# Two steps of attention values at a time, and a routing table ahead of two conditioning products

## The reference, cut to what matters

```python
    order = jnp.argsort(flat_e)
    ...
    xb = h_pad[slot_tok].reshape(n_blocks, MOE_BLOCK, d)
    def run_block(args):
        xe, e = args
        return (jax.nn.silu(xe @ w_gate[e]) * (xe @ w_up[e])) @ w_down[e]
```

```python
def ada_mod(cond, w, b):
    m = jnp.dot(jax.nn.silu(cond), w) + b
    return jnp.split(m, 3, axis=-1)
```

```python
p = softmax(MLA_SCALE * (q_nope . k_nope + q_rot . k_rot))   # over 1280 keys
o = p @ v                                                    # 64 columns a head
```

## Time and profile before

| | |
|---|---|
| median of 3 runs | 2509.48 us (2509.85, 2502.32, 2509.48) |
| the profiled execution's own time | 2505.39 us |
| its span | 2503.5 us |
| mean granted TensorE clock | 0.959 |
| TensorE busy | 2298.8 us, 92% |
| VectorE busy | 1526.8 us, 61% |
| ScalarE busy | 1186.9 us, 47% |
| GpSimd busy | 373.4 us, 15% |

### The profile page before, as it was taken

The page is one execution under the profiler, slowest core; times in us unless marked ns, Lnnn a source line. Parts: engine busy times, 40 slices in busy tenths (PEclk is TensorE's granted clock), DMA queues, the critical chain, the costliest instruction groups (busy, mean ns, idle before and its releaser), DMA issues.

```text
span 2503.5 us, 27157 instructions
## 1 busy us (share of the span) xinstructions
PE 2298.8 (92%) x10924; PEld 1710.5 (68%) x10924; DVE 1526.8 (61%) x1874; ACT 1186.9 (47%) x1666; POOL 373.4 (15%) x258
## 2 busy tenths in 40 slices
PE   6998789798699999999989999898999998899998
PEld 5766565475388888888768876654555467688876
DVE  5776257543699999999881125846455647533475
ACT  3255246521388888888753154425444522312221
POOL 2000012000111111111100000011555633000014
PEclk9999899899799999999989998998999999999999
DMA  3201010115899999999761110010000032111131
GB/s 119 67 19 49 0 68 1 68 76 215 354 362 387 379 387 396 394 393 378 303 207 50 49 35 1 1 38 1 1 4 31 17 126 76 52 52 51 55 156 51
DMA packets 100953, 342.19 MB, mean 137 GB/s; under 512 B 23356, under 2 KB 48741, under 8 KB 73176
## 3 DMA queue, kind: packets, MB, share of 16 engines
q1 hardware_dynamic: 89176, 318.89, 33.9%
q0 software_dynamic: 10448, 17.28, 1.9%
q10 hardware_dynamic: 1200, 4.24, 0.4%
HBM read 323.54 MB, written 33.60 MB: 143 GB/s over the span
## 4 chain that ended last, share of the span: by engine, by line
PE 81%; DVE 10%; ACT 5%; DMA 3%; issue 1%; SPq 0%; DVEq 0%; POOL 0%; ACTq 0%; POOLq 0%
PE psm L230 77%; DVE mem L953 1%; PE psm L1722 1%; ACT mem L1143 1%; DMA mem<-in_ada_w_dram 1%; PE psm L1073 1%; DVE r L337 1%; DMA mem<-in_w_in_dram 1%; DVE mem L2735 1%; ACT mem L1109 1%; PE psm L1745 1%; PE psm L464 1%; DMA mem<-in_odd_w_out_dram 1%; DVE small L3002 0%; PE psm L1442 0%
## 5 line engine op out<-in xcount | busy, mean ns | idle before, releaser
L230 PE MATMUL psm<-r,r 128*128 128x512 f32 (+3 forms) x7294 | 1750.4, 398 | 77.6 <-DVE r L337 18.0
L230 PEld LDWEIGHTS psm<-r,r 128*128 128x128 f32 (+2 forms) x7294 | 1371.9, 191 | 453.5 <-issue 61.7
L337 DVE TENSOR_TENSOR r<-mem,r 128x1024 fp32r<-128x1024 f32 x448 | 526.1, 1222 | 185.9 <-ACT r L328 180.8
L328 ACT ACTIVATE r<-mem 128x1024 fp32r<-128x1024 f32 x448 | 441.7, 1053 | 34.6 <-DMA mem<-in_w_in_dram 22.2
L230 PE MATMUL psm<-mem 128*64 128x128 f32 (+13 forms) x2230 | 357.9, 437 | 35.1 <-ACT mem L816 10.1
L230 PEld LDWEIGHTS psm<-mem 128*64 128x64 f32 (+6 forms) x2230 | 168.3, 163 | 156.7 <-issue 88.7
L3210 POOL TENSOR_TENSOR mem<-mem 128x1024 f32<-128x1024 f32 x63 | 153.9, 2443 | 176.3 <-ACT mem L3165 175.6
L3165 ACT ACTIVATE mem<-psm 128x512 f32<-128x512 f32 x160 | 95.3, 596 | 145.7 <-PE psm L230 138.2
L3002 DVE TENSOR_REDUCE small<-psm 128x1 f32<-128x1280 f32 x64 | 95.3, 1489 | 102.4 <-PE psm L230 102.2
L230 PE MATMUL psm<-mem,cst 128*128 128x512 f32 (+4 forms) x274 | 114.0, 634 | 23.9 <-ACT mem L924 5.5
L265 ACT ACTIVATE small<-small 128x1 f32<-128x1 f32 (+3 forms) x26 | 7.7, 295 | 236.8 <-DVE small L374 151.6
(11 more groups left out here) (338 smaller groups left out, 1745.9 us busy)
## 6 DMA issues: line engine op xcount, KB each, us to landing
mem<-in_exp_w_gate_dram SPq DMA_DIRECT2D x64, 1024.0 KB, 7.5
mem<-in_exp_w_up_dram SPq DMA_DIRECT2D x64, 1024.0 KB, 7.8
mem<-in_exp_w_down_dram SPq DMA_DIRECT2D x64, 1024.0 KB, 7.3
mem<-in_ada_w_dram SPq DMA_DIRECT2D x16, 1024.0 KB, 14.3
mem<-in_odd_w_in_dram SPq DMA_DIRECT2D x10, 1024.0 KB, 5.4
mem<-in_even_w_in_dram SPq DMA_DIRECT2D x9, 1024.0 KB, 5.4
mem<-in_x_dram SPq DMA_DIRECT2D x16, 512.0 KB, 7.2
mem<-in_w_in_dram SPq DMA_DIRECT2D x8, 1024.0 KB, 5.3
```

The costliest lines, as they stand in the source:

```text
L230: return p.e.matmul(o, l, r, start=start, stop=stop, skip_group_check=True)
L328: p.e.activation(h, mem(kb + 8, [R * n])[:, w * q:w * q + w], ACT.Copy).then_inc(*self.hi_done.up(i, q))
L337: p.e.tensor_tensor(l, mem(kb + 8, [R * n])[:, w * q:w * q + w], h.bitcast(F32), SUB).then_inc(*self.lo_done.up(i, q))
```

## The change

Four things move; no product, copy or DMA is added or taken away.

1. `latent_tensor` multiplies the values of two steps at a time, at odd steps only: at odd t those of t - 3 and t - 2, then the sums that are due.
2. As the sums may come a step later, ScalarE's and VectorE's work at the end of each half (L3173 to L3190) moves from step t = 13, 23, ... to t = 14, 24, ...
3. On TensorE the router's "pos" and "tot" stand ahead of conditioning product 8, and the table ahead of products 10 and 11.
4. On ScalarE the last `ada_rows` stands behind the splits of weight pieces 0 and 1. On GpSimd the clearing of the second gather buffer, which waits for product 11, stands behind the first gather.

```diff
@@ norm2_tensor
-            ada_tensor(p, 4, 9)
+            ada_tensor(p, 4, 8)
@@ router_scalar
-            for g in range(3):
+            for g in range(2):
                 ada_rows(p, g)
@@ rows_pool
-            p.wait_ge(*ada_pe.at(11))
-            p.e.memset(XGB[1], 0.0).then_inc(*moe_pool.up(1))
@@ experts_pool
             gather(p, 0)
+            p.wait_ge(*ada_pe.at(11))
+            p.e.memset(XGB[1], 0.0).then_inc(*moe_pool.up(1))
             gather(p, 1)
@@ experts_scalar
-            for i in range(3):
+            for i in range(2):
                 WE.split_scalar(p, i)
+            ada_rows(p, 2)
+            WE.split_scalar(p, 2)
@@ latent_tensor
-                if 0 <= t - 2 < 80:
-                    values_tensor(p, t - 2)
-                if 0 <= t - 3 < 80 and STEPS[t - 3][2] in (4, 9):
-                    sums_tensor(p, t - 3)
+                if t % 2:
+                    for k in (t - 3, t - 2):
+                        if 0 <= k < 80:
+                            values_tensor(p, k)
+                    for k in (t - 4, t - 3):
+                        if 0 <= k < 80 and STEPS[k][2] in (4, 9):
+                            sums_tensor(p, k)
@@ latent_scalar and latent_vector (the same index in each of their lines)
-                if 0 <= t - 4 < 80 and STEPS[t - 4][2] == 9:
+                if 0 <= t - 5 < 80 and STEPS[t - 5][2] == 9:
@@ tensor
-            ada_tensor(p, 9, 12)
+            ada_tensor(p, 8, 10)
             table_tensor(p)
+            ada_tensor(p, 10, 12)
```

More of the change, by code:

```diff
@@ L3167, in latent_scalar @@
                     beside_scalar(p, t)
-                if 0 <= t - 4 < 80 and STEPS[t - 4][2] == 9:
-                    hp, half, i = STEPS[t - 4]
-                    p.wait_ge(*ml_pe.at("sum", t - 4))
+                if 0 <= t - 5 < 80 and STEPS[t - 5][2] == 9:
+                    hp, half, i = STEPS[t - 5]
+                    p.wait_ge(*ml_pe.at("sum", t - 5))
                     if hp + half:
@@ L3182, in latent_vector @@
                     beside_vector(p, t)
-                if 0 <= t - 4 < 80 and STEPS[t - 4][2] == 9:
-                    hp, half, i = STEPS[t - 4]
+                if 0 <= t - 5 < 80 and STEPS[t - 5][2] == 9:
+                    hp, half, i = STEPS[t - 5]
                     y = YM[:, hp, 512 * half:512 * half + 512]
-                    p.wait_ge(*ml_pe.at("pv", t - 4))
+                    p.wait_ge(*ml_pe.at("pv", t - 5))
                     p.wait_ge(*ml_act.at("r", hp, half))
```

## The result

| | before | after |
|---|---|---|
| median of 4 runs each | 2507.97 us (2502.32 to 2509.85) | 2490.48 us (2489.08 to 2492.07) |
| ratio | | 0.9935, 95% interval 0.9918 to 0.9952 |
| profiled execution: own time / span | 2505.39 / 2503.5 us | 2492.07 / 2490.2 us |
| TensorE busy | 2298.8 us | 2292.1 us |
| latent attention, first scores to first product behind it | 280.47 us | 268.62 us |

A forecast was written before the change was run, and what follows sets the result against it. TensorE, busy for 92% of the span, was taken as the bound. Attention -9 and routing -2 gave -11 us: 2494.4 from the profiled execution, 2498.5 from the median, middle 2496 us, range 2486 to 2508.

The forecast's parts named there:

- Part 2, the stalls: Latent attention: the long TensorE waits at steps 25 and 45 go, -5.9 us each; steps 61 to 68 give -1.2.
- Rival A: Attention: the stalls only move, one long wait with low clock returning per twenty steps; about 2508 us, chance 0.21.
- Part 1, pairs with items: Attention: a pair with two items takes 6.47 us against 6.34, +3.4 us over 26 pairs; the start loses 0.9.
- the item by that pace is 0.58, and 0.19 us is the switch to values: Attention, item to values: of 0.77 us the item takes 0.58, leaving a 0.19 us switch that pairing saves.
- Two zeros of part 1: Attention: pairing values changes nothing in seven pairs with tops, nor in the last ten steps, there within 1 us.
- Weight loads between sets of values: Attention: by a skill rule the second set waits for its load, about 4 us worse; measured rows showed less.
- Part 3, the routing: Router to first expert: moving the table earlier starts the first expert product at 673 to 675, -2 us.
- an earlier first product is worth its whole lead: Experts: TensorE bounds them from the first product on, so that product's lead, -2 us, counts in full.
- it follows the one-hot matrices within 1 to 2 us: Router: the table comes 1 to 2 us behind the one-hot matrices, so indices are ready about 7.5 us earlier.
- Product 10 at 654 keeps the DMA of piece 3 where it is: Between router and experts: conditioning product 10, at 654, leaves the DMA of weight piece 3 unmoved; effect nothing.
- Rival C: Attention: 0.46 us waits in 26 pairs lower TensorE's clock, making the kernel slower, about 2522 us; chance 0.09.
- Rival B: Attention: the short waits are hidden, pairs gain 0.33 us each instead of losing 0.13; about 2484 us, chance 0.10.

The follow-up runs named there:

- vector_shift_only: The kernel before, with only VectorE's division and gate at the end of a half one step later; 2491.15 us (one run), attention 267.16 us.
- items_apart: The kernel after, with the two items of a pair on either side of the two sets of values; 2496.19 us, ratio 0.9962, attention 270.82 us.
- mixed_ten_first: The kernel after, with values paired only where no item waits and the table behind conditioning product 10; 2488.00 us, ratio 0.9930.
- warm_table: The kernel after, with three spare fp32 products filling TensorE's idle time ahead of the table; 2491.84 us, ratio 0.9942.
- ten_first: The kernel after, with the table behind conditioning product 10 instead of 9; 2488.93 us, ratio 0.9931.
- single_ten_first: The kernel after, with values one step at a time and the table behind conditioning product 10; 2488.70 us, ratio 0.9934, attention 267.19 us.
- routing_only: The kernel before, with only the new routing order and the attention unchanged; 2504.88 us, ratio 0.9996, attention 283.42 us.
- after_again: The kernel after, unchanged, run again beside later kernels on the same chip; 2490.72 us, ratio 0.9943, attention 268.64 us.
- pairs_only: The kernel before, with only the values two steps at a time and the end of a half unmoved; 2513.39 us, ratio 1.0038, attention 288.43 us.
- warm_table_rows_first: The kernel after, with three spare products ahead of the table and ScalarE's last conditioning rows ahead of the weight splits; 2489.12 us, ratio 0.9928.
- shift_only: The kernel before, with only the end of a half one step later on ScalarE and VectorE; 2493.45 us, ratio 0.9955, attention 267.18 us.

## Why the prediction came out, step by step

**Part 2, the stalls: right in mechanism and size.** Two times -5.9 us was the term. Ten undisturbed steps, from tops to tops, take 33.77 us in before and 34.07 in after. Those with steps 25 and 45 took 39.75 us each in before, 6.0 over that, and take 34.07 in after, nothing over it: -6.0 each. Those with steps 61 to 68 took 36.17 us and take 34.98, so what they are over went from 2.4 to 0.9 us: -1.5 (predicted -1.2). vector_shift_only shows the cause directly. Rival A did not come: from step 4 on no wait is over 0.54 us.

**Part 1, pairs with items: right.** A pair was to take 6.47 us; it takes 6.46. The start was to lose 0.9 and lost 0.86. But the two parts of the difference were both put too high, by 0.25 and 0.29 us, and cancel: the saving was put at 0.33 (0.19 ahead of the values, 0.14 behind) and is 0.08 by items_apart, and the wait was put at 0.46 and is 0.17 in the profile. The step that failed is "the item by that pace is 0.58, and 0.19 us is the switch to values". The whole interval from item to item, 2.43 us at steps 1 and 2, holds both, and since it went into the sum as measured, the sum came out right. The row itself had said 0.20 us of wait.

**Two zeros of part 1: mis-sized.** The pairs with tops were counted as 0: a pair of steps with tops takes 6.46 us instead of 6.62, so -0.16 in each of seven, -1.1. The step that failed is "only the values' place changes": two sets of values in a row save their 0.15 us there too, and no item waits. The last ten steps were counted as 0, less than 1 us either way: five pairs take 5.13 instead of 5.22 us, and a wait of 0.43 us on ScalarE's exponential is gone; with it -1.1 in all. Together they are most of the difference between the predicted -9 and the measured -11.85 us; the rest is some 0.4 us in the stalls and 0.4 us in the pairs. mixed_ten_first confirms these sizes: without the pairs with items the attention is 265.01 us, 2.2 shorter than with no pairs, which is the -1.1 twice; with them it is 3.6 longer, which is 26 x 0.11 plus 0.86 (over ten steps a pair with items costs 0.11 us more than two single steps).

**Weight loads between sets of values.** Two sets of values take 1.87 us from start to start, against 2.02 for two apart. The prediction weighed the rule of the Trainium skill's page "TensorE: Matmul & The Clock Gate", section "The mechanism", by which a load into row groups in use would wait. The second set costs less than the first, so no wait as after a switch shows here, as three sets in a row had told.

**Part 3, the routing: the first product right, its path wrong in three places, its worth wrong.** The first product came at 673.48, inside 673 to 675, and -2 us was predicted where the trace gives -2.6. But of the lead, 1.7 us outlives the first expert and only 0.3 to 0.5 us shows at the attention. The step that failed there is "an earlier first product is worth its whole lead": half of it goes into products at the lower clock, and where the rest goes stays open. The path:
- The table: "it follows the one-hot matrices within 1 to 2 us" failed. It takes 5 us, and the gather is issued at 660.5 instead of about 657, because TensorE idles 3.06 us and then works at 1.2 GHz (0.50 to 0.51). The clock was counted in the attention and not here; warm_table shows it.
- The last conditioning rows, which "leave at about 664 to 665" behind ScalarE's splits, came at the right time in part by luck: the copy starts at 663.9 and the DMAs at 664.6, but what the copy waits for last is product 11 (0.38 us, TensorE), which the slow table had pushed back. Both delays happen to end together; in warm_table, without the slow table, the splits alone hold it up.
- "Product 10 at 654 keeps the DMA of piece 3 where it is" failed: product 10 now stands behind the table and the DMA is issued 7 us later. ten_first, single_ten_first and mixed_ten_first undo it, and no gain shows that lasts in all three (the attention starts 1105.4, 1108.4 and 1108.5 us behind the tokens, against 1108.5 in after).

The rows' landing, which no row gave, was taken at 672; it was 671.3. The gather landed at 670 and not at 665. That cost nothing, as warm_table shows: there the expert's transposes start at 664.67, and the first product is no earlier.

**Rival C, slower by the clock: refuted.** The Trainium skill's page "TensorE: Matmul & The Clock Gate", section "A second HAM failure mode: psum-queue depth-cycling", warns of short idles between groups of products. Here 27 waits of 0.17 to 0.54 us left the granted clock at 1.00 over 256 us, so this trace does not show it. The prediction had argued so from the short waits of the earlier trace rows. Its other support, the 2.1 us wait that left the clock at 1.00, did not come again in routing_only. Rival B could not have come: without its wait a pair saves 0.08 us and not 0.33, some 2 us in all and not 9.

**The rest of the 17.5 us.** The traces give -13.3 us; the prediction gave -11 against the profiled execution. The other 4.2 us come from both ends: the median of before is 2.6 us above its profiled execution, and that of after is 1.6 us below its own. The choice of the middle between both bases was a guess about this. The base itself moves: beside the later kernels the median of before was 2507.78, 2508.16 and 2503.22 us, and after_again gained 12.5 us on its own where after had gained 17.5. The attention's 11.85 us, which came again to 0.02 us in after_again, is the firm part. The rest, among it how near 2496 came to 2490.5, is in part chance.

## What to carry to other kernels

An engine that works in order and serves the one that bounds the kernel should have long work that nobody waits for (here a division and a gate) behind the short work that the bound engine waits for. One step of slack was worth 13 us here, more than any saving in the bound engine's own row. Each half of such a change should be run alone, as one may carry all of the gain and the other cost some. Grouping like products saved time here only where the buffers between them came free in time. When a long wait is removed, the slow products behind it go too. The same test has to be made wherever the change creates a new idle time, however small the chain around it looks. And a lead at one product is not yet a gain at the end: it should be followed to a landmark far behind, in more than one trace of the same kernel.

## What the runs showed of the hardware

- Two sets of fp32 values in a row take 1.87 us, against 2.02 apart; twelve fp32r scores in a row take 3.26 us, against 3.20 for twice six. So putting two steps together saves TensorE some 0.09 us: 0.15 on the values, less 0.06 on the scores.
- In the attention of after, 27 waits of 0.17 to 0.54 us cost TensorE no clock. Behind the longer ones: 1.68 us was followed by 1.2 GHz once and once not (items_apart), some 2.1 us once and once not (step 65 of routing_only and of before), 2.59 us all four times (before and routing_only), 3.2 and 3.9 us all three times (pairs_only), 3.06 us ahead of the table as well.
- After the wait ahead of the first expert the clock came back 5.9 us behind the first product in after and 3.1 us behind it in ten_first, with TensorE busy in both. That alone moved the start of the second expert by 1.4 us, nearly as much as the routing's change was worth there.
- The conditioning rows, 4 small writes to DRAM while the DMA engines were full (a share of 1.01 to 1.02), were waited for until 6.6 to 7.4 us behind the issue of the first (after, routing_only, warm_table, warm_table_rows_first, ten_first). Once the gather is early, this is what ScalarE's copy for the first expert waits for.
- VectorE's lo of 96x1024 takes 1.21 us with no addition of GpSimd beside it, 2.2 to 2.3 us with 1.2 to 1.4 us of one beside it, and 3.40 us with 2.3 us of one beside it (before, shift_only, after).
